# The final norm's gain row loaded by ten transfers on ten semaphores, in a transformer block on one core

## The chip, the cores and the metric

One Trainium2 chip, one core of it, and one launch. The metric is the device time of the kernel in microseconds (us), lower is better. Three runs of the kernel before gave 469.45, 469.94 and 470.28 us, with a median of 469.94. Engines are named as the profile names them: PE is the matrix engine (TensorE), PEld its weight load, DVE is VectorE, ACT is ScalarE, POOL is GpSimd, and SP is SyncE, which here only issues DMA transfers and waits. A `q` behind a name (DVEq, SPq) is the sequencer of that engine, which runs waits, branches and DMA issues.

## The reference

256 tokens of 1024 values pass one layer and a final norm, all in float32:

- x is normalised and projected; a differential attention branch and a gated delta-net branch are gated, merged, projected, and added to x;
- x is normalised again and goes through a mixture of 32 experts (4 groups of 8, the best 2 of the best group for each token), each with gate and up matrices 1024x256 and a down matrix 256x1024; the weighted sum is added to x;
- the last step, the one that the change touches:

```python
def rms_norm(x, gain):
    xf = x.astype(jnp.float32)
    y = xf * lax.rsqrt(jnp.mean(xf * xf, axis=-1, keepdims=True) + EPS)
    return (y * gain.astype(jnp.float32)).astype(x.dtype)
...
    return rms_norm(x, norm_final_gain)
```

`norm_final_gain` is one row of 1024 float32 values, 4096 bytes.

## The kernel before

There is no tiling framework: each engine has a function that writes its instructions in order (`sync_program`, `gpsimd_program`, `scalar_program`, `tensor_program`, `vector_program`), and engines meet only by semaphores. A DMA transfer adds 16 to its semaphore when it has landed, a compute instruction adds 1. Tokens lie on the 128 partitions, in two tiles (t = 0, 1).

The first 230 us are the two branches. Then the 32 experts run as 32 units, eight groups of four. The weights of an expert are three transfers of 1 MB (gate, up, down), issued by SP into seven slots of SBUF. SP issues a reload when the slot is used up (`gateup_used`, `experts_used`), in the loops of lines 394 to 418. The last expert's transfers are those of lines 423, 403 (for the one before it) and 429, in two halves of 512 KB.

Behind them, at line 433, SP issues the load of the gain row: one transfer of 128 partitions, each of which gets the same 4096 bytes, so 512 KB. Its semaphore is `gfin_loaded`, and it is gated by `gateup_used` >= 27 because it goes into a slot's memory. SP then issues only the two stores of the output (line 440), each when its half-rows are ready (`out_left_ready`, `out_right_ready`).

On ACT, DVE and PE all expert code stands in `by_count` (lines 810 to 822): nested If and Else over the largest number of tokens that an expert has, with four versions of the loops. Here the first version runs, and at its end each engine branches (line 813) over the other three.

Behind that branch stands the end of the kernel on DVE (lines 2026 to 2035). For each tile t it waits for ACT's first sum of squares (`squares_done`), makes the mean of it (line 2029), multiplies the left half with the gain (line 2030, which ACT or POOL will scale), waits for ACT's root (line 746), takes the reciprocal (line 2032), and scales and multiplies the right half (line 2034). POOL scales the left half of tile 0 (line 499), ACT that of tile 1 (line 754), behind POOL's by `out_left_ready`. ACT makes the sums of squares from PSUM (line 739) as PE's last matmuls (line 1297) deliver them, and these stand inside the branch on ACT.

Nine semaphores are used for early loads and are then idle: `first_loaded` (it has 16 when its load has landed), `x_loaded0` (16), `x_loaded1` (16), `lambda_loaded` (64), `blocks_loaded` (16), `vectors_loaded` (64), `inverse_loaded` (32), `A_stored` (32), `consts_loaded` (48). The waits for them in the first 260 us are of the form "at least", and all of them are passed long before line 433.

Of the kernel before, what the change touches and what calls it, by code (L numbers as in the profile page):

```python
# [22 lines left out]
P = 128  # L23
# [23 lines left out]
EARLY = (4, 2)  # L47
WARM = 5
BIG = 1e30
LAMBDA_INIT = 0.2  # L50


# [240 lines left out]
def sync_program(sp, c, io):  # L293

    s = c.s
# [124 lines left out]
    e, i, had = EXPERTS - 1, loads - 1, sum(EARLY) * HID  # L420
# [6 lines left out]
    for half, sem in enumerate((f"down{e % SLOTS}", "last_down")):  # L427
# [2 lines left out]


    sp.wait_ge(s["gateup_used"], EXPERTS - SLOTS + 2)
    sp.dma_start(c.gfin, io["norm_final_gain"].rearrange("(a d) -> a d", a=1).partition_broadcast(P)
                 .rearrange("p a d -> p (a d)")).then_inc(s["gfin_loaded"], 16)

    outv = io["out"].rearrange("b (t p) d -> p (b t) d", p=P)
# [373 lines left out]
def by_count(eng, largest, windows):  # L810

    (m0, n0), (m1, n1), (m2, n2), (_, n3) = PATHS
    with eng.If(largest <= m0):
        windows(n0)
    with eng.Else():
        with eng.If(largest <= m1):
            windows(n1)
        with eng.Else():
            with eng.If(largest <= m2):
                windows(n2)  # L820
            with eng.Else():
                windows(n3)
# [628 lines left out]
def vector_program(v, c, io):  # L1451
    s = c.s
    n = [0]

    def chain(ins):
        n[0] += 1
        ins.then_inc(s["dve_chain"], 1)

    def settle():
        v.wait_ge(s["dve_chain"], n[0])  # L1460
# [7 lines left out]
    def side(name):  # L1468
        v.wait_ge(s["side_ready"], SI[name] + 1)
        return c.side[side_pair(name)]  # L1470
# [235 lines left out]
    def maxima(qt):  # L1706

        nk = P * (qt + 1)
        for m in range(2):
            ps = side(f"s{qt}{m}").rearrange("p (h k) -> p h k", h=H)  # L1710
            chain(v.memset(ps[0:CHUNK, :, nk - CHUNK:nk], -BIG))
            settle()
# [35 lines left out]
    def new_values(n_):  # L1748

        rows = slice(CHUNK * (n_ % 2), CHUNK * (n_ % 2) + CHUNK)  # L1750
        dst = c.vn[n_ // 2][rows]
        u = c.u[rows, n_ // 2]
        if n_ == 0:
            v.tensor_copy(dst, u).then_inc(s["vn_ready"], 1)
        else:
            ps = side(f"ws{n_}")[rows, 0:512].rearrange("p (h f) -> p h f", h=H)
            v.tensor_tensor(dst, u, ps, ALU.subtract).then_inc(s["vn_ready"], 1)
            v.wait_ge(s["vn_ready"], n_ + 1)
            v.sem_inc(s[f"side_free{side_pair(f'ws{n_}')}"], 1)
# [24 lines left out]
    settle()  # L1784
    chain(v.tensor_scalar(c.lamw[:, 0:1], c.lamw[:, 0:1], LAMBDA_INIT, None, ALU.subtract))
    new_values(0)
# [13 lines left out]
    def head_norm(squares, ss, sq_flat, root):  # L1800

        v.wait_ge(s[squares], 1)
        chain(v.tensor_reduce(ss, sq_flat.rearrange("p (a f) -> p a f", a=8), AX_X, ALU.add))
        settle()
        v.tensor_scalar(ss, ss, 1.0 / P, EPS, ALU.mult, ALU.add).then_inc(s[root], 1)
        v.wait_ge(s[root], 2)
        chain(v.reciprocal(ss, ss))
        settle()
    new_values(3)
    attended(1)  # L1810

    chain(v.tensor_scalar(c.subln, c.subln, 1.0 - LAMBDA_INIT, None, ALU.mult))
    head_norm("oa_squares", c.ra, c.flat["Yb"], "oa_root")
# [31 lines left out]
    v.wait_ge(s["iota_ready"], 1)  # L1845
    chain(v.tensor_scalar(c.below, c.below, -BIG, None, ALU.mult))
    v.wait_ge(s["rank_masks_ready"], 1)
# [175 lines left out]
                alone(grp, ends(grp), False)  # L2023
    by_count(v, largest, windows)

    v.wait_ge(s["gfin_loaded"], 16)
    for t in range(NT):
        v.wait_ge(s["squares_done"], 2 * t + 1)
# [83 lines left out]
def build(nc, io):  # L2112
    with ExitStack() as ctx:
        c = lay_out(nc, ctx)

        c.A_stored = nc.dram_tensor("stored_A", (4 * H * (CHUNK * CHUNK + CHUNK),), F32, kind="Internal").ap()
        c.inverses_stored = nc.dram_tensor("stored_inverses", (2, 2 * H, P, BLOCK), F32, kind="Internal").ap()
        block = ctx.enter_context(nc.Block())

        @block.sync  # L2120
        def _(sp):
            sync_program(sp, c, io)

        @block.gpsimd
        def _(pool):
            gpsimd_program(pool, c, io)

        @block.scalar
        def _(act):
            scalar_program(act, c, io)  # L2130

        @block.tensor
        def _(pe):
            tensor_program(pe, c, io)

        @block.vector
        def _(v):
            vector_program(v, c, io)
# [24 lines left out]
```

## Time and profile before

| what | value |
|---|---|
| median of 3 runs | 469.94 us (469.45 to 470.28) |
| the profiled execution's own time | 470.17 us |
| its span, first to last instruction | 468.4 us |
| PE busy | 437.4 us (93%) |
| DVE, ACT, POOL busy | 202.0, 122.8, 12.5 us |
| mean granted TensorE clock | 0.971 of 2.4 GHz |
| bytes by SP's queue (q1) | 135.22 MB, 73.1% of 16 engines' span |

The span leaves out 1.8 us of the profiled execution's time. Busy shares are averages over stages with different limits, so the table says little about the last 30 us, where the change lies. For these the chain of waits and the timeline are read: each line of the chain is a start in us from the span's start, a length in us, and what was running or being waited for.

### The profile page before, as it was taken

The page shows a single profiled execution, that of the slowest core. Times are in us where ns is not written, and L with a number is a line of the kernel's source. Part 1 is how long each engine was busy: PE and PEld are TensorE (multiplying, and loading weights), DVE is VectorE, ACT ScalarE, POOL GpSimd, SP SyncE. Part 2 cuts the span into 40 slices and gives each one's busy share as a digit, 9 for nine tenths or more (in the row PEclk, how much of TensorE's full clock was granted, in tenths as well). Part 3 has the DMA queues.
Part 4 walks back from the last instruction along what each step waited for, and adds up shares of the span by engine and source line. Part 5 has one row for each costly group of instructions (what it writes and reads, how often), then busy time and mean ns, then how long its engine had stood idle before and what let it go on. Part 6 is the DMA issues. An engine that isn't in the chain of part 4 may idle for free.

```text
span 468.4 us, 10279 instructions
## 1 busy us (share of the span) xinstructions
PE 437.4 (93%) x4337; PEld 328.4 (70%) x4337; DVE 202.0 (43%) x568; ACT 122.8 (26%) x313; POOL 12.5 (3%) x37
## 2 busy tenths in 40 slices
PE   9999999999999999999999999999997977797683
PEld 8885688874888888888645777768684745665351
DVE  1376367996343551613200654344463123413224
ACT  5002522001132312220012733324242212312134
POOL 6010100000000000000000000000000000000001
PEclk9999999999999999999999999999999787989898
DMA  8969957706504042255598989999999999999982
GB/s 310 407 212 332 411 193 254 278 26 211 183 11 171 23 157 62 118 180 181 195 421 372 348 333 422 418 417 420 419 420 419 422 418 418 421 420 421 415 332 99
DMA packets 38193, 136.87 MB, mean 292 GB/s; under 512 B 9600, under 2 KB 9920, under 8 KB 26240
## 3 DMA queue, kind: packets, MB, share of 16 engines
q1 hardware_dynamic: 33776, 135.22, 73.1%
q10 hardware_dynamic: 4368, 0.95, 1.1%
q8 instruction: 36, 0.59, 0.5%
q14 instruction: 13, 0.11, 0.1%
HBM read 134.59 MB, written 1.57 MB: 291 GB/s over the span
## 4 chain that ended last, share of the span: by engine, by line
PE 65%; DMA 20%; DVE 9%; SPq 3%; issue 2%; ACT 1%; POOLq 0%; ACTq 0%; DVEq 0%
PE ps L890 23%; DMA arena<-in_moe_w_up 12%; PE ps L1268 8%; PE ps L1131 6%; PE ps L1146 6%; DMA ring<-in_moe_w_up 6%; PE ps L1321 3%; PE ps L1311 3%; PE ps L1226 2%; DVE arena L1645 2%; DVE arena L1642 2%; SPq L398 2%; DMA arena<-in_w_in 2%; PE ps L917 2%; PE ps L1276 1%
## 5 line engine op out<-in xcount | busy, mean ns | idle before, releaser
L890 PE MATMUL ps<-arena 128*128 128x256 f32 (+1 forms) x640 | 157.0, 403 | 0.4 <-DMA arena<-in_w_in 0.4
L890 PEld LDWEIGHTS ps<-arena 128*128 128x128 f32 x640 | 119.8, 190 | 29.9 <-issue 14.9
L1268 PE MATMUL ps<-arena 128*32 128x128 f32 x1072 | 41.9, 299 | 13.1 <-DMA arena<-in_moe_w_up 12.9
L1268 PEld LDWEIGHTS ps<-arena 128*32 128x32 f32 x1072 | 32.5, 117 | 20.5 <-DMA arena<-in_moe_w_up 15.3
L1268 PE MATMUL ps<-ring,arena 128*32 128x128 f32 x912 | 34.1, 293 | 7.1 <-DMA ring<-in_moe_w_up 7.1
L703 ACT ACTIVATE gains<-ps 32x256 f32<-32x256 f32 x62 | 23.3, 376 | 56.2 <-PE ps L1311 55.8
L1268 PEld LDWEIGHTS ps<-ring,arena 128*32 128x32 f32 x912 | 26.8, 114 | 12.2 <-DMA ring<-in_moe_w_up 8.1
L1947 DVE TENSOR_TENSOR masks<-ps,masks 128x64 f32<-128x64 f32 x32 | 7.2, 225 | 59.9 <-ACT masks L684 59.7
L1963 DVE COPY arena<-ps 32x256 f32<-32x256 f32 x62 | 25.8, 416 | 11.2 <-PE ps L1311 10.3
L1146 PE MATMUL ps<-arena 128*128 128x512 f32 x64 | 28.3, 595 | 0.0
L1226 PE MATMUL ps<-masks,arena 128*128 128x128 f32 x224 | 28.3, 287 | 0.0
L1226 PEld LDWEIGHTS ps<-masks,arena 128*128 128x128 f32 x224 | 26.9, 200 | 1.8 <-issue 1.8
L1131 PE MATMUL ps<-arena 128*128 128x256 f32 x128 | 28.0, 379 | 0.0
L1131 PEld LDWEIGHTS ps<-arena 128*128 128x128 f32 x128 | 24.2, 190 | 3.3
L1146 PEld LDWEIGHTS ps<-arena 128*128 128x128 f32 x64 | 11.9, 190 | 13.4 <-issue 13.4
L588 ACT ACTIVATE arena<-ps 128x1024 f32<-128x1024 f32 x7 | 7.2, 1023 | 50.9 <-PE ps L890 31.4
L1311 PE MATMUL ps<-arena,masks 128*32 128x256 f32 x256 | 17.0, 382 | 0.1
L690 ACT ACTIVATE masks<-ps 64x64 f32<-64x64 f32 x32 | 6.9, 217 | 37.8 <-PE ps L1276 37.8
L1311 PE MATMUL ps<-ring,masks 128*32 128x256 f32 x240 | 15.9, 382 | 0.0
L1837 DVE TENSOR_TENSOR arena<-arena,ps 128x1024 f32<-128x1024 f32 x4 | 4.9, 1221 | 24.7 <-PE ps L1131 24.7
L1321 PE MATMUL ps<-arena,rw 128*128 128x512 f32 x28 | 15.3, 630 | 0.0
L1932 DVE TENSOR_TENSOR arena<-ps,small 128x512 f32<-128x512 f32 x8 | 5.5, 692 | 22.7 <-PE ps L1226 21.1
(286 smaller groups left out, 453.6 us busy)
## 6 DMA issues: line engine op xcount, KB each, us to landing
arena<-in_w_in SPq DMA_DIRECT2D x9, 2048.0 KB, 7.9
arena<-in_moe_w_gate SPq DMA_DIRECT2D x16, 1024.0 KB, 24.0
arena<-in_moe_w_up SPq DMA_DIRECT2D x16, 1024.0 KB, 25.2
arena<-in_moe_w_down SPq DMA_DIRECT2D x16, 1024.0 KB, 23.9
ring<-in_moe_w_down SPq DMA_DIRECT2D x15, 1024.0 KB, 26.6
ring<-in_moe_w_gate SPq DMA_DIRECT2D x14, 1024.0 KB, 23.3
ring<-in_moe_w_up SPq DMA_DIRECT2D x14, 1024.0 KB, 24.8
arena<-in_w_out SPq DMA_DIRECT2D x2, 2048.0 KB, 7.8
```

Of the source, the lines that this page charges most:

```text
L398: sp.dma_start(flat[slot], src[:, e, :].rearrange("p a f -> p (a f)")).then_inc(s[f"gateup{slot}"], 16)
L703: last = act.activation(stacked(c, i, q), down_out(c, i, q), ACT.Copy)
L890: last = pe.matmul(out, lhs, rhs, start=(k == 0 and (i > 0 or part % 2 == 0)), stop=(k == KD - 1), skip_group_check=(i == 0))
L917: last = pe.matmul(out(ps, i, m), lhs(t, h, m), rhs(t, h, m), start=True, stop=True)
L1131: last = pe.matmul(blk(branch_out(c, half), b, TOK), w[:, k, (4 * half + b) * P:(4 * half + b + 1) * P], yT[:, k, :], start=(k == 0), stop ...
L1146: last = pe.matmul(c.ps[:, 4 + 2 * t + half, :], mg, w[:, k, :], start=(k == 0), stop=(k == KD - 1))
L1226: last = pe.matmul(gather_out(c, k), c.h2[:, t, k, :], c.oh[:, t, :], start=(t == 0), stop=(t == NT - 1))
L1268: last = pe.matmul(c.ps[ROWS * q:ROWS * (q + 1), i % 2, 0:P], c.Hg[:, k, ROWS * i:ROWS * (i + 1)], w[:, :, start:start + 127:2], start=(k ...
L1311: last = pe.matmul(down_out(c, i, q), c.actT[i % 2][:, kk * ROWS:(kk + 1) * ROWS], c.down_w[slot][:, kk, 256 * q:256 * (q + 1)], start=(kk ...
L1321: last = pe.matmul(y_out(c, half, t), c.S_e[:, t * P:(t + 1) * P], c.Y[half], start=False, stop=False, skip_group_check=True)
L1642: chain(v.tensor_tensor(outer, c.block[:, w:BLOCK, j:j + 1].to_broadcast([BLOCKS, n_, w]), c.inverse[:, j:j + 1, 0:w].to_broadcast([BLOCKS ...
L1963: last = v.tensor_copy(stacked(c, i, q), down_out(c, i, q))
```

## The change

The one transfer becomes ten. The first nine load 1, 3, 4, 5, 8, 10, 12, 6 and 15 partitions (64 together), each on one of the nine idle semaphores, and the tenth loads the other 64 partitions on `gfin_loaded`. All stand at the same place of SP's program, behind the same gate. DVE waits for all ten before the final norm. The total is 512 KB as before.

```diff
+GAIN_ROWS = ((1, "first_loaded", 16), (3, "x_loaded0", 16), (4, "x_loaded1", 16), (5, "lambda_loaded", 64), (8, "blocks_loaded", 16), (10, "vectors_loaded", 64),
+             (12, "inverse_loaded", 32), (6, "A_stored", 32), (15, "consts_loaded", 48))
...
     sp.wait_ge(s["gateup_used"], EXPERTS - SLOTS + 2)
-    sp.dma_start(c.gfin, io["norm_final_gain"].rearrange("(a d) -> a d", a=1).partition_broadcast(P)
+    row = 0
+    for n, sem, _ in GAIN_ROWS:
+        sp.dma_start(c.gfin[row:row + n], io["norm_final_gain"].rearrange("(a d) -> a d", a=1).partition_broadcast(n)
+                     .rearrange("p a d -> p (a d)")).then_inc(s[sem], 16)
+        row += n
+    sp.dma_start(c.gfin[row:], io["norm_final_gain"].rearrange("(a d) -> a d", a=1).partition_broadcast(P - row)
                  .rearrange("p a d -> p (a d)")).then_inc(s["gfin_loaded"], 16)
...
     by_count(v, largest, windows)
 
+    for _, sem, had in GAIN_ROWS:
+        v.wait_ge(s[sem], had + 16)
     v.wait_ge(s["gfin_loaded"], 16)
```

## Rows read from the trace of the kernel before

**Rows 1.** Page, part 2: mean busy share of the 16 DMA engines, slices of 11.7 us.
```profile
DMA  8969957706504042255598989999999999999982
```

**Rows 2.** Chain of waits from 456 us: start us, us, what.
```profile
458.18 0.42 DVE gains L1955
458.60 1.98 issue
460.59 0.02 DVEq L2028
460.61 0.06 issue
460.67 0.15 DVE small L2029
...
460.85 0.70 DVE arena L2030
...
461.69 1.62 POOLq L2113
...
463.33 0.04 ACTq L753
463.37 0.05 issue
```

**Rows 3.** Timeline of SP: start us, us, engine line op out<-in.
```profile
9.67 1.39 SPq L339 DMA_DIRECT2D small<-in_gdn_dt_bias  x1
11.10 0.63 SPq L339 DMA_DIRECT2D gains<-in_diff_subln_gain  x1
...
23.80 0.58 SPq L339 DMA_DIRECT2D gains<-in_diff_lambda_q  x1
...
27.07 0.47 SPq L349 DMA_DIRECT2D rw<-in_moe_w_group  x1
...
30.99 4.95 SPq L351 DMA_DIRECT2D small<-in_norm_ffn_gain  x1
...
424.60 2.21 SPq L423 DMA_DIRECT2D ring<-in_moe_w_gate  x1
...
435.88 4.44 SPq L429 DMA_DIRECT2D arena<-in_moe_w_down  x1
440.36 4.30 SPq L433 DMA_DIRECT2D arena<-in_norm_final_gain  x1
```

**Rows 4.** Page, part 6: DMA issues, count, KB each, median us from issue to landing.
```profile
out_y<-arena SPq DMA_DIRECT2D x2, 512.0 KB, 3.6
arena<-in_norm_final_gain SPq DMA_DIRECT2D x1, 512.0 KB, 17.3
gains<-in_diff_subln_gain SPq DMA_DIRECT2D x1, 64.0 KB, 13.8
small<-in_gdn_dt_bias SPq DMA_DIRECT2D x1, 2.0 KB, 15.0
```

**Rows 5.** Line 429: us from issue to landing of its two transfers.
```profile
DMA to landing us min/median/max: 20.6/21.0/21.5
```

**Rows 6.** Line 813: the branch out of the If; ns min/median/max.
```profile
L813 PEldq COMPARE_BRANCH  x2: 89/1878/3666, 268.1 to 458.7; - x2
L813 DVEq COMPARE_BRANCH  x2: 47/51/55, 268.9 to 457.8; - x2
```

**Rows 7.** Timeline of ACT and DVE at the end.
```profile
459.92 0.19 ACT L739 ACTIVATION_READ_ACCUMULATOR arena<-ps 128x1 f32 x1
...
461.46 0.15 DVE L2032 RECIPROCAL small<-small 128x1 f32<-128x1 f32 x1
```

**Rows 8.** Lines 1492, 1493, 515: semaphore instructions of DVE and a 48-partition issue; ns.
```profile
L1492 DVEq EVENT_SEMAPHORE  x1: 21/21/21, 16.5 to 16.5; - x1
L1493 DVEq EVENT_SEMAPHORE  x1: 50/50/50, 16.6 to 16.6; - x1
L515 ACTq DMA_DIRECT2D cst_in<-in_gdn_conv_w x1: 338/338/338, 1.5 to 1.5; - x1
```

## The prediction, as made before the changed kernel was run

> **What bounds the kernel now.** I read the page's DMA slices first, then the chain of waits over the last 14 us, then SP's timeline for the transfers, then the landings. The slices show nine tenths or more from about 290 us to 445 us [rows 1]: the expert weights' bytes set the time there, and the gain row is the last thing behind them. From 450 us on the chain is made of compute [rows 2]. Its last part is: DVE's copy of the last expert's output ends at 458.60, then 1.98 us of "issue" (DVE waits for nothing that the profile shows), then the wait at line 2028, the mean (460.67), the left half's product (460.85 to 461.54), then POOL's scaling of the left half, ACT's, and the stores. The reader is to see that DVE's program from line 2026 on stands on the path that sets the end, and that the gain row does not: it is issued at 440.36 and lands 17.3 us later, at 457.7 [rows 3, 4], and DVE takes up line 2028 at 460.59 only. The slack is 2.9 us.
>
> Why is DVE late? ACT's first sum of squares is complete at 459.92 + 0.19 = 460.11 [rows 7], so the wait at 2028 was 0.48 us overdue when DVE came to it. Ahead of it stands the branch at 457.8 over the other three versions, 0.05 us by itself on DVE; on PE the branch of the same line lasts 3.67 us, from 458.7 [rows 6]. I read the 1.98 us as DVE getting its code from behind the branch. The Trainium skill says so as a rule (Runtime: NRT & Kernel Launch, section "Instruction fetch mechanics"): a taken branch to code outside the window that is held must fetch that page first, and the engine stands still. The rows agree, and this makes what follows the branch on DVE exposed: by the other reading the added waits would cost nothing.
>
> **The change part by part.**
>
> *The nine waits on DVE.* They are added between the branch and line 2028. How are waits packed? At lines 1489 to 1495 DVE has four waits (lines 1490 to 1493) ahead of one instruction. The rows show two semaphore instructions there, of 21 ns and 50 ns [rows 8]. Lines 750 to 753 on ACT have three waits and the chain shows one semaphore instruction of 0.04 us [rows 2]. So an instruction takes one wait itself, a semaphore instruction of 21 ns carries one, and a longer one carries two. Before, lines 2026 and 2028 were two waits: one semaphore instruction and one on line 2029. After, there are eleven: one on line 2029, ten in five semaphore instructions. Price: 0.02 + 0.06 = 0.08 us for the single one (460.59 to 460.67), 0.04 + 0.05 = 0.09 us for a double one (463.33) [rows 2]; DVE's double one is 0.012 us longer than ACT's, so 0.10. Sum: 5 x 0.09 to 0.10 less 0.08 = +0.37 to +0.43 us. Bounds: 0 if the waits pass during the 1.98 us, and 10 x 0.08 - 0.08 = +0.72 us if each wait is an instruction of its own. I take +0.4, from the rows nearest to it. All of it goes on: the product at 460.85 ends at 461.54 and DVE's work behind it is in order, POOL starts behind it, ACT waits for POOL, the stores wait for both [rows 2]. Queued behind the waiting instructions is the whole final norm of both tiles. If all ten transfers are there, nothing else changes.
>
> *The first piece on SP.* It inherits gate and place of the old transfer. That one's issue lasted 4.30 us, and the one before it 4.44 [rows 3]; whether this is the gate or a queue that is full, the first piece bears it again and ends at about 444.7.
>
> *The other nine issues.* A short issue takes 0.5 to 0.6 us with others still in flight: seven of them, with the gaps behind them, fill 23.80 to 27.54, so 0.53 us each [rows 3]. An issue of 48 partitions costs 0.34 us on ACT [rows 8]. So nine take 9 x 0.53 = 4.8 us, to 449.5. Behind them on SP stand only the stores, 14 us later: this costs nothing as long as the last issue is over by about 457. Other bound: while the queue is full an issue takes 2.1 to 2.2 us even for a quarter of the size (2.21 at 424.60), once even 4.95 for a transfer of 4 KB behind two with many small pieces [rows 3]. Nine at 2.15 would be 19 us. I take 0.53, since the pieces are short, and keep the other end for the rival.
>
> *The landing.* The weights ahead are not moved. The last of them lands at 435.88 + 20.6 = 456.4 [rows 3, 5], the gain row 1.2 us behind it. The pieces queue there too, the bytes are the same. What each landing costs beside its bytes: two small loads issued 1.4 us apart behind the same backlog land at 9.67 + 15.0 = 24.7 and 11.10 + 13.8 = 24.9, so 0.2 us apart [rows 3, 4]. Nine more such steps are 1.8 us: the last landing is 457.7 to 459.5, before 460.6. Cost nothing; the cover is DVE's branch, and each us that the last piece is later than about 460.9 is a us of the total.
>
> Which engines carry the pieces no row shows. The Trainium skill (DMA: Bandwidth & Descriptors, section on why a DMA increments its semaphore by 16) says that a transfer goes over as many of the 16 engines, at most 16, as divides its outer size, and the lowest-numbered ones. By it the first DMA engine gets one row of each of eight pieces, a quarter of the single row, and 4 rows of the last 64, so 12.25 instead of 8. With 1.2 us for 8 rows that is 0.65 us more, a landing at 458.3 instead of 457.7, and the sum stays as it is.
>
> *The reused semaphores.* Their earlier waits ask for "at least" and are passed 180 us or more before; no instruction is added there. Nothing.
>
> **Sum.** +0.4 us on the span (468.4 to 468.8), +0.4 on the profiled execution's own 470.17, so 470.6. That execution is 0.23 above the median 469.94 of the runs, so for the median I expect 470.3 us. What this measurement can tell from no change is 0.2%, 0.94 us; +0.4 (0.09%) is below that.
>
> **The rivals.**
>
> *Hidden waits* (chance 0.12). If the 1.98 us is a wait that the added ones can run inside, the time stays 469.9. For it: the profile names no reason for the stall. Against it: the sum of squares was there at 460.11, and the branch on PE.
>
> *A full queue holds the pieces back* (0.14, the rival on the slower side). Place: SP's issues from 444.7. Price: 2.15 us each until the weights are through at 456.4, so five of them (to 455.4), then four at 0.53 to 457.5. The last piece lands on an empty queue after 3.6 us, as the stores of 512 KB do [rows 4], so at 461.1 at the latest; a later throttle (one more 4.3 us as at 435.88) makes it 465. It decides once the landing is behind 460.9: 0.2 us in the first form, 4.1 in the second, and I price this rival at the middle, 2.1 us with the 0.4 of the waits, 472.0. For it: the issues of 2.1 to 6.3 us that fill SP's timeline from 413 on. Against it: the seven quick ones from 23.80.
>
> *Each landing costs more than a queue shows* (0.03). If each of nine landings cost 0.9 us, the last would be at 465.8, 4.9 late: 475.2. Against it: the 0.2 us above.
>
> *Code placement* (0.03 each way). Five more instructions on DVE behind the branch, nine on SP; if they pass an edge at which code is fetched, DVE stands once more for about 2 us (472.3), or comes earlier (by the 0.48 us that it was late, 469.5, and no faster unless PE's and ACT's shares move too).
>
> That the ten do not do what one did is not among them: the rows 0 to 63 and 64 to 127 are all covered, each once.
>
> **How the numbers follow.** Forecast 0.65, its own range 469.5 to 471.1 (0 to 0.72, and 0.4 us for the spread of the runs). Within 0.2%: 0.61 of the forecast's 0.65, the hidden waits' 0.12, and of the queue rival's mild form 0.02: 0.75. Slower: 0.03 of the forecast, 0.12 of the queue rival, 0.03 of the landings and 0.03 of the code: 0.21. Faster: 0.03 of the code and 0.01 of the forecast, 0.04. The range reaches up to the queue rival's price and below to the fastest run: 469.3 to 471.9.
>
> **What would show each step.** Between the branch and line 2029 five DVE semaphore instructions of 0.05 us in place of one, and line 2029 at about 461.1. Nine short SP issues from 444.7 to 449.5, and the longest landing among the ten at 457.7 to 459.5. The interval from line 2029 to the end of the span the same as before, 7.7 us. Wrong if: SP issues of 2 us or more between the pieces and DVE's wait ending with a landing; or more than five semaphore instructions on DVE.

## The result, and the profile after

The changed kernel takes 471.94 us (median of 4 runs, 471.63 to 472.46) against 469.90 for the kernel before (469.45 to 470.28). The ratio is 1.0040, with a 95% interval of 1.0028 to 1.0052: 0.4% slower, +1.3 to +2.4 us. The forecast was 470.3 and "within 0.2%". The time lies beyond that bound and at the very end of the range, 471.9. The profiled execution took 471.64 us with a span of 469.9, so +1.5 us on the 470.17 and 468.4 of before. It is one of the two shortest of the four runs, so the rows account for 1.5 us, not for the median's 2.0. In what follows a median is of all executions; one of 548 to 876 us in each of e2, e7, e9, e10 and e12 ran in a slow state, counts in that median, and is left out of the ratio.

The chain of waits of the changed kernel from 435 us on (start us, us, what). Lines 1294, 1962, 2037 and 2038 are lines 1287, 1955, 2028 and 2029 of before.

```profile
435.56 22.08 DMA arena<-in_moe_w_down
457.65 0.04 issue
457.69 1.08 PE ps L1294 x8
458.77 0.02 issue
458.80 0.06 DVE gains L1962
458.86 2.79 issue
461.65 0.05 DVEq L2034
461.70 0.06 issue
461.75 0.05 DVEq L2034
461.80 0.05 issue
461.85 0.05 DVEq L2034
461.90 0.05 issue
461.95 0.05 DVEq L2035
462.00 0.05 issue
462.05 0.05 DVEq L2037
462.10 0.05 issue
462.15 0.15 DVE small L2038
462.30 0.03 issue
462.33 0.70 DVE arena L2039
```

Two things differ from [rows 2]. First, five double semaphore instructions stand ahead of the mean, 0.05 us each and 0.10 apart. The mean starts 0.50 us after the first of them, where it was 0.08: +0.42 us. Second, all of it starts at 461.65 and not at 460.59: +1.06 us. Together 1.48 us, and that is the whole of the span's 1.5: from the mean to the end of the span it is 7.7 us in both.

Where is the 1.06 from? The chain now ends in a transfer that was not in it: the last half of the last expert's down matrix, issued at 435.56, lands at 457.65. The weights' two landings, by the line that issues them in the changed kernel (us from issue to landing; [rows 5] has those of before, 20.6 for the last half, which landed at 456.43):

```profile
DMA to landing us min/median/max: 22.1/22.5/22.8
```

The last half is 1.2 us late. PE waits for it with the second half of line 1294, which ends at 458.77. Before, these matmuls had both halves' data and ended at 457.71:

```profile
456.68 1.04 PE ps L1287 x16
457.71 0.02 issue
```

PE is 1.06 us later, so DVE's last copy is, so is its branch, and the 2.8 us behind the branch are then paid from there. The branches in the changed kernel (ns min/median/max, first and last start us; those of before are in [rows 6]):

```profile
L820 PEldq COMPARE_BRANCH  x2: 89/1886/3682, 267.8 to 459.3; - x2
L820 DVEq COMPARE_BRANCH  x2: 47/51/55, 268.6 to 458.8; - x2
```

From DVE's branch to its next instruction it is 2.8 us in both (457.8 to 460.59 before, 458.8 to 461.65 after).

SP in the changed kernel (start us, us, engine line op out<-in xcount), and the last piece of the gain row on the page (KB, us from issue to landing):

```profile
433.37 6.48 SPq L431 DMA_DIRECT2D arena<-in_moe_w_down  x2
439.90 7.11 SPq L437 DMA_DIRECT2D arena<-in_norm_final_gain  x9
447.05 0.52 SPq L440 DMA_DIRECT2D arena<-in_norm_final_gain  x1
```

```profile
arena<-in_norm_final_gain SPq DMA_DIRECT2D x1, 256.0 KB, 12.0
```

Ten pieces are issued within 7.7 us, none of them behind a stall of 2 us or more, and the one issued last lands at 459.05, 2.6 us before DVE asks. The landings of the other nine are not in the profile, but none of DVE's five semaphore instructions stands still. So the gain row is not waited for. It harms the weights ahead of it. The windows around 451 us show how (us from:to, length; busy us of PE, PEld, DVE, ACT, POOL with counts; granted clock; DMA share, GB/s). Before:

```profile
445.00:451.00 6.00, 6.00 (x93) 3.63 (x96) 1.25 (x3) 1.19 (x4) 0.00 (x0) 1.00 1.03 407
451.00:453.00 2.00, 1.83 (x42) 1.11 (x38) 1.34 (x4) 1.25 (x5) 0.00 (x0) 1.00 0.90 355
```

The changed kernel:

```profile
445.00:451.00 6.00, 6.00 (x101) 3.74 (x103) 1.25 (x3) 1.42 (x5) 0.00 (x0) 1.00 1.02 406
451.00:453.00 2.00, 1.82 (x49) 1.22 (x45) 1.35 (x4) 1.19 (x4) 0.00 (x0) 1.00 0.96 248
453.00:455.00 2.00, 1.01 (x36) 0.73 (x28) 0.51 (x2) 0.91 (x2) 0.00 (x0) 1.00 0.72 218
```

Until 451 us nothing differs, though all ten pieces are issued by 447.6. From then on the DMA engines are as busy as before and move 248 GB/s in place of 355. Bytes per busy share, 394 before (355 / 0.90) and 258 after, is the number that I follow through the experiments: packets take 1.5 times as long. No instruction of DVE, ACT or PE explains it; their busy times in this window are the same within 0.1 us (DVE 1.34 and 1.35, ACT 1.25 and 1.19, PE 1.83 and 1.82).

The trace also has each packet's size and duration, and there the two loads can be told apart: the gain row goes in 128 packets of 4096 bytes, the weights of this stretch in packets of 2048 and 8192. In the kernel before, the gain row's packets run from 450.9 to 457.2 us, among the weights', the last of which ends at 455.9. So both are in flight together there too, and it does no harm. A weight packet of 2048 bytes that starts between 451 and 453 us takes 87 ns in the median there and 126 in the changed kernel; one of 8192 bytes takes 314 and 488. It is the weights' own packets that slow.

### The profile page after: what moved, and what is told of

Same layout as the page of the kernel before. It is cut to its first block, busy times and chain, and to the rows that moved or that the text cites. A ratio compares the mean times of both kernels' runs of the same rounds, so it can differ in the third digit from the quotient of the medians.

```text
span 469.9 us, 10292 instructions
## 1 busy us (share of the span) xinstructions
PE 441.1 (94%) x4337; PEld 330.9 (70%) x4337; DVE 201.9 (43%) x568; ACT 122.9 (26%) x313; POOL 12.5 (3%) x37
## 4 chain that ended last, share of the span: by engine, by line
PE 67%; DMA 19%; DVE 8%; issue 2%; SPq 1%; ACT 1%; POOLq 0%; ACTq 0%; DVEq 0%
PE ps L897 23%; PE ps L1275 9%; DMA arena<-in_moe_w_up 6%; DMA ring<-in_moe_w_up 6%; PE ps L1138 6%; PE ps L1153 6%; DMA arena<-in_moe_w_down 5%; PE ps L1233 4%; PE ps L1318 4%; PE ps L1328 3%; DVE arena L1652 2%; DVE arena L1649 2%; DMA arena<-in_w_in 2%; PE ps L924 2%; PE ps L1283 1%
## 5 line engine op out<-in xcount | busy, mean ns | idle before, releaser
L1275 PE MATMUL ps<-arena 128*32 128x128 f32 x1072 | 43.4, 307 | 12.5 <-DMA arena<-in_moe_w_up 12.1
L1233 PEld LDWEIGHTS ps<-masks,arena 128*128 128x128 f32 x224 | 28.0, 207 | 2.0 <-issue 2.0
L1233 PE MATMUL ps<-masks,arena 128*128 128x128 f32 x224 | 29.4, 293 | 0.0
L1153 PEld LDWEIGHTS ps<-arena 128*128 128x128 f32 x64 | 11.9, 190 | 13.4 <-issue 13.4
```

The source lines that it names most:

```text
L1153: last = pe.matmul(c.ps[:, 4 + 2 * t + half, :], mg, w[:, k, :], start=(k == 0), stop=(k == KD - 1))
L1233: last = pe.matmul(gather_out(c, k), c.h2[:, t, k, :], c.oh[:, t, :], start=(t == 0), stop=(t == NT - 1))
L1275: last = pe.matmul(c.ps[ROWS * q:ROWS * (q + 1), i % 2, 0:P], c.Hg[:, k, ROWS * i:ROWS * (i + 1)], w[:, :, start:start + 127:2], start=(k ...
```

## The experiments

Two costs are to be explained: the waits (+0.42) and the late weights (+1.06). The theories on the second, by their letters:

- P: transfers of fewer than 128 partitions slow whatever is in flight beside them (first put more narrowly: because a piece's rows are neighbouring partitions).
- N: the number of transfers or of packets does it. S: the ten semaphores do. U: small pieces put more rows on some DMA engines than on others. Q: one source row read by many small transfers. R: chance, the late landing is one execution's.
- On the waits, H: they are hidden in the stall behind the branch.

Every experiment was timed beside the kernel before on the same chip; its times there were medians of 470.13 to 470.29 us. The edits of e2, e3, e4, e7 and e11 are shown against the changed kernel, those of e5, e6, e8, e9, e10 and e12 against the kernel before; where only new lines are shown they stand in place of the load of the gain row.

**e1, the changed kernel again** (no edit).

> The changed kernel once more, for a second profile. Theory W (small pieces slow the weight packets that are still under way, and the five added DVE semaphore instructions cost 0.4 us): the last down half lands about 1.2 us later than in the kernel before, packets in the stretch around 451 to 454 us take 1.3 to 1.6 times as long, the time is about 2 us above the kernel before. Rival R (the slow packets were chance in one profiled execution): they are gone in this profile, and the time is about 0.5 us above the kernel before.

471.98 us (471.46 to 472.55) against 470.13, ratio 1.0038 (1.0026 to 1.0049). The last half lands after 21.8 us, and the window of 451 to 453 us has 252 GB/s at 0.98. R is refuted: another execution, the same two findings. (e1 to e4 share a chip, e5 to e8 a second, e9 to e12 a third; the late weights appear on all three.)

**e2, only the waits.** One transfer as before; nine waits for values already reached.

```diff
-    row = 0
-    for n, sem, _ in GAIN_ROWS:
-        sp.dma_start(c.gfin[row:row + n], ...).then_inc(s[sem], 16)
-        row += n
-    sp.dma_start(c.gfin[row:], ... .partition_broadcast(P - row) ...
+    sp.dma_start(c.gfin, ... .partition_broadcast(P) ...
...
-        v.wait_ge(s[sem], had + 16)
+        v.wait_ge(s[sem], had)
```

> One transfer as before; DVE keeps the nine waits, at values that the nine semaphores have long reached. Theory W: +0.4 us against the kernel before (five semaphore instructions of 0.10 us in place of one of 0.08), the last down half lands as before. Rival H (waits hidden in the stall behind the branch): 0.0 us.

470.96 us, ratio 1.0016 (1.0001 to 1.0030): +0.8 us with an interval of 0.05 to 1.4, which holds the 0.4 and just excludes 0. The weights are on time (20.3 us; 334 GB/s at 0.85, so 393 per share). The chain behind its branch:

```profile
457.37 3.02 issue
460.39 0.05 DVEq L2029
...
460.78 0.05 DVEq L2032
460.83 0.05 issue
460.89 0.15 DVE small L2033
```

The waits run behind the stall, not in it: 0.50 us from the first to the mean again. H is refuted.

**e3, ten transfers on one semaphore.**

```diff
-                     ... .then_inc(s[sem], 16)
+                     ... .then_inc(s["gfin_loaded"], 16)
...
-    for _, sem, had in GAIN_ROWS:
-        v.wait_ge(s[sem], had + 16)
-    v.wait_ge(s["gfin_loaded"], 16)
+    v.wait_ge(s["gfin_loaded"], 16 * (len(GAIN_ROWS) + 1))
```

> The ten transfers as in the change, all on gfin_loaded, DVE waits once for 160. Theory W: about 1.6 us above the kernel before, 0.4 below the change; the last down half lands late as in the change. Rival S (the nine reused semaphores or their waits are what costs): as the kernel before, 0.0 us.

471.54 us, ratio 1.0024 (1.0011 to 1.0037). The weights are as late as in the change (22.1 us; 239 GB/s at 0.97). S is refuted. On the same chip it is 0.44 us below e1, from which it differs by the nine semaphores and their waits alone: the third reading of 0.4.

**e4, ten slices of columns**, each over all 128 partitions (102 columns, 408 bytes a row), on the ten semaphores.

```diff
+    gain = io["norm_final_gain"].rearrange("(a d) -> a d", a=1)
+    for i, sem in enumerate([g[1] for g in GAIN_ROWS] + ["gfin_loaded"]):
+        a, b = 102 * i, 102 * (i + 1) if i < len(GAIN_ROWS) else D
+        sp.dma_start(c.gfin[:, a:b], gain[:, a:b].partition_broadcast(P) ... .then_inc(s[sem], 16)
```

> Ten transfers of all 128 partitions, each 102 (the last 106) columns wide, on the ten semaphores, with the ten waits. Theory P (it is the shape that costs: few partitions, so that several DMA engines write where one does otherwise): weights land as before, +0.4 us for the waits alone. Rival N (it is the number of transfers): the last down half lands 1.2 us late here too, +1.6 us or more.

470.60 us, ratio 1.0012 (0.9998 to 1.0026), so +0.5 us, in line with the waits alone, though the interval reaches 0. The profile has the waits: from the first of the five semaphore instructions (460.35) to the mean (460.85) it is 0.50 us. The last half lands after 20.3 us. As many transfers as in the change and ten times the rows of the one transfer of before, and the weights are on time: N is refuted. The window has 294 GB/s at 0.83, 354 per share, but here the gain row goes in packets of 408 bytes, so that number can't be compared; the weights' packets of 2048 bytes can, and take 84 ns. One thing is not equal: the ten issues take 13.4 us and end at 453.5, six us later than in the change. e12 is the counterpart without that gap.

**e5, eight transfers of 16 neighbouring partitions**, one semaphore. By the rule that the prediction quotes, 16 rows are one for each of the 16 DMA engines, and U needs them uneven.

```diff
+    for i in range(8):
+        sp.dma_start(c.gfin[16 * i:16 * i + 16], ... .partition_broadcast(16) ...).then_inc(s["gfin_loaded"], 16)
```

> Eight transfers of 16 neighbouring partitions each, one semaphore, one wait for 128. Every DMA engine gets one row of every transfer, 8 in all as in the kernel before. Theory P (several engines write into neighbouring partitions at once, and that slows every packet in flight): packets from 451 us on are slow, the last down half lands 1 us or more late, +1.2 to +1.6 us. Rival U (it is that the low-numbered engines get more rows than the others): all engines get the same here, the weights land at 456.1 to 456.4 as before, 0.0 us.

471.23 us, ratio 1.0019 (1.0009 to 1.0029); landing after 21.6 us. U is refuted. The whole of this trace is 0.4 us later, so the window catches less of it (334 GB/s, but at a share of 1.07: 312). From 452 to 454 us its weight packets of 2048 bytes take 134 ns, where the kernel before has 84.

**e6, the same with every eighth partition** (rows i, i+8, ... in one transfer).

```diff
+        sp.dma_start(c.gfin[i:P:8], ... .partition_broadcast(16) ...).then_inc(s["gfin_loaded"], 16)
```

> Eight transfers of 16 partitions that lie 8 apart (i, i+8, ...), one semaphore, one wait. As many transfers, rows and engines as with neighbouring partitions. Theory P: with each transfer spread over all partitions the packets are faster than with neighbouring ones, the last down half lands within 0.5 us of the kernel before's 456.4. Rival N (the number of small transfers, or k of 16 with one row each, costs): the same lateness as with neighbouring partitions.

471.31 us, ratio 1.0022 (1.0012 to 1.0032); 21.9 us; 256 GB/s at 1.00. As late as with neighbouring rows. My narrow form of P fell here: which partitions a piece has does not matter.

**e7, rows of x as the source.** The ten pieces take their rows from 128 different rows of x, so the gain is left out and x stands in its place; one semaphore.

```diff
-        sp.dma_start(c.gfin[row:row + n], io["norm_final_gain"]... .partition_broadcast(n) ...
+        sp.dma_start(c.gfin[row:row + n], io["x"][0, row:row + n, :]).then_inc(s["gfin_loaded"], 16)
...
+    sp.dma_start(c.gfin[row:], io["x"][0, row:P, :]).then_inc(s["gfin_loaded"], 16)
```

> The ten transfers with one semaphore, but each partition loads a row of x of its own (4096 bytes each, 128 different rows) in place of the one gain row; the final norm therefore multiplies with x and not with the gain. Theory P (destination): as with the gain row, the last down half lands about 1.2 us late, +1.6 us. Rival Q (several engines read the same 4 KB of HBM at once): with rows of their own the packets are fast again, the weights land at 456.4, 0.0 us.

471.58 us, ratio 1.0027 (1.0017 to 1.0037); 22.0 us; 269 GB/s at 1.02. Q is refuted.

**e8, two transfers of 64 partitions**, one semaphore.

```diff
+    for i in range(2):
+        sp.dma_start(c.gfin[64 * i:64 * i + 64], ... .partition_broadcast(64) ...).then_inc(s["gfin_loaded"], 16)
```

> Two transfers of 64 partitions, one semaphore, one wait for 32. Theory P: each engine writes 4 neighbouring rows, two engines share what one writes in a transfer of 128; a part of the lateness, 0 to 0.6 us. Rival N (number of transfers): 2 of 10, at most 0.2 us. Rival U: 0.0 us.

471.68 us, ratio 1.0033 (1.0023 to 1.0043): +1.5 us where I had expected 0 to 0.6. Two transfers cost as much as ten on one semaphore (e3, 1.4). The landings are the latest of all kernels, and the window is slow:

```profile
DMA to landing us min/median/max: 22.5/22.6/22.8
```

```profile
451.00:453.00 2.00, 1.97 (x58) 1.58 (x54) 0.89 (x3) 1.19 (x4) 0.00 (x0) 1.00 1.04 272
```

So of what these runs vary, what counts is that a transfer has fewer than 128 partitions (1 to 64 here; nothing between 64 and 128 was run); how many pieces there are does not.

**e12, two transfers of 128 partitions**, halves of the columns: the counterpart to e8 (edit on the kernel before).

```diff
+    for i in range(2):
+        sp.dma_start(c.gfin[:, 512 * i:512 * i + 512], ... .partition_broadcast(P) ...).then_inc(s["gfin_loaded"], 16)
```

> Two transfers of all 128 partitions, each half of the columns, one semaphore and one wait for 32: as many transfers and bytes as in two of 64 partitions. Theory P: packets at full speed, last down half at 456.1 to 456.4, 0.0 us. Rival N (two transfers in place of one): +1.5 us as with 64 partitions.

470.17 us, ratio 0.9994 (0.9980 to 1.0007): no difference. Its landings and its window:

```profile
DMA to landing us min/median/max: 20.5/20.9/21.4
```

```profile
451.00:453.00 2.00, 1.96 (x49) 1.31 (x48) 0.43 (x2) 0.66 (x3) 0.00 (x0) 1.00 0.96 372
```

388 per share against e8's 262, with the same count of transfers and of bytes, and weights on time against 2 us late. The weights' packets of 2048 bytes take 87 ns in e12 and 132 in e8. (Its profiled execution, 471.41, is the longest of the nine behind the ratio, and PE was already 1.1 us behind at 451 us, ahead of the window; of it only landing, window and packets are used.)

**e9, the two transfers of 64 behind the weights.** SP waits for the last half first.

```diff
+    sp.wait_ge(s["last_down"], 16)
+    for i in range(2):
+        sp.dma_start(c.gfin[64 * i:64 * i + 64], ... .partition_broadcast(64) ...).then_inc(s["gfin_loaded"], 16)
```

> Two transfers of 64 partitions as before, but SP issues them only when the last down half has landed, so that no weight packet is in flight beside them. Theory P (gain packets with another assignment of engines to partitions slow the weight packets beside them): the last down half lands at 456.1 to 456.4 as in the kernel before; the gain row lands about 3.6 us after that, near 460.1, just before DVE asks; 0 to +0.3 us against the kernel before, 1.3 us below the same two transfers issued early. Rival L (a split load costs by itself, whatever is beside it, or DVE's end is late for another reason): +1.5 us as when issued early.

The weights are on time, as P says (20.5 us). The time is not: 471.73 us, ratio 1.0028 (1.0015 to 1.0041), +1.4 us where I had expected 0 to 0.3. The chain, SP and the window of the pieces in e9:

```profile
458.05 0.42 DVE gains L1958
458.47 3.50 issue
461.97 0.02 DVEq L2031
```

```profile
456.51 1.15 SPq L437 DMA_DIRECT2D arena<-in_norm_final_gain  x2
```

```profile
457.50:460.00 2.50, 1.88 (x7) 0.91 (x6) 0.91 (x3) 1.44 (x4) 0.00 (x0) 1.00 0.76 218
```

The pieces are slow even among themselves: 287 per share, and 212 ns for a packet of 4096 bytes, which takes 159 in the kernel before. Their last packet ends at 460.25 and they land until 460.96. DVE meanwhile stands 3.50 us behind its branch in place of the 1.98 of [rows 2], and once it goes on it waits for nothing more. The 1.5 us move from the weights to the stall. The instruction queue shows where they go. Packets, MB and share of DMA, first in the kernel before from 457.8 to 459.5 us, then in e9 from 457.6 to 459.7, where the data queue is all that moves:

```profile
q14 instruction: 1, 0.01, 1.8%
```

```profile
q1 hardware_dynamic: 142, 0.49, 79.8%
```

Before, the 8 KB packet of instructions starts at 458.75, 1.0 us behind DVE's branch, and so it does in the other profiles with that branch (1.0 to 1.3). In e9 the branch is at 457.62 and the packet starts at 459.79, 2.2 us behind it, when most of the pieces' packets are through; DVE's next instruction follows 2.2 us behind that start, before 1.8. So the fetch is late, by 1.2 us at its start. That it stands behind the pieces' packets fits and is argued. No run has one transfer of 128 partitions at this place, so whether the form of the pieces matters here, or any transfer would do it, is open.

**e10, DVE's final norm inside the branch** (the kernel before; lines 2026 to 2035 moved to the end of `windows`, each version with its own copy). It asks whether the stall is the fetch behind the branch.

```diff
+        v.wait_ge(s["gfin_loaded"], 16)
+        for t in range(NT):
+            ... (the loop's body, unchanged)
...
     by_count(v, largest, windows)
-    v.wait_ge(s["gfin_loaded"], 16)
-    for t in range(NT):
-        ...
```

> The kernel before, with DVE's final norm moved to the end of each version inside the If, so that no branch stands ahead of it. Theory B (DVE stands after the branch until its code is there, 0.46 us past the sum of squares): line 2029's instruction starts at 460.2 in place of 460.67, and the time is 0.3 to 0.5 us lower. Rival O (DVE is held by something else): 0.0 us.

The stall is gone. ACT and DVE in e10:

```profile
459.65 0.19 ACT L739 ACTIVATION_READ_ACCUMULATOR arena<-ps 128x1 f32 x1
...
459.96 0.15 DVE L2027 TENSOR_SCALAR small<-small 128x1 f32<-128x1 f32 x1 [1.62 <-ACT arena L739]
```

DVE's mean starts 0.12 us after ACT's sum (459.84), where it was 0.56 late [rows 2, 7]. The Trainium skill states the rule (Runtime: NRT & Kernel Launch, "Instruction fetch mechanics": a taken branch out of the pages that are held forces a fetch before execution goes on); this run agrees, with 0.44 us of lateness gone and no packet of q14 between 457.8 and 463 us.

Yet the kernel is not faster: 471.11 us, ratio 1.0011 (0.9999 to 1.0023). The mean is 0.71 us earlier than before (459.96 against 460.67), but the reciprocal behind it only 0.34 (461.12 against 461.46 [rows 7]): it waits for ACT's root, and ACT is at its second sum of squares until 460.70. So the two stores are issued 0.3 us earlier, and they land later. The stores on the page, and the instruction queue from 463 to 469 us (packets, MB, share), in e10:

```profile
out_y<-arena SPq DMA_DIRECT2D x2, 512.0 KB, 4.2
```

```profile
q14 instruction: 4, 0.03, 2.1%
```

Before, the stores took 3.6 us [rows 4] and that window had 2 packets of q14 (and one of q8, which in e10 starts at 462.79, ahead of the window). DVE's branch is now at 463.05, and its packet of instructions at 464.0 or 464.3, beside ACT's: the fetch is not saved but moved, to where the stores run. They take 4.2 us here and 3.9 in e11, and 3.4 to 3.8 in the twelve others. That the fetch is what slows them fits and is not separated. The moving of the code bought nothing.

**e11, the same edit on the changed kernel.**

> The changed kernel with the same move. The last down half stays late (about 457.6), but the five semaphore instructions can run right behind DVE's last copy, before ACT's sum of squares at about 460.53. Theory B: the mean starts near 460.6 in place of 462.15, 1.4 to 1.6 us below the changed kernel, about level with the kernel before. Rival O: 0.4 us below at most.

471.31 us, ratio 1.0013 (1.0000 to 1.0026), span 468.9. Its chain:

```profile
435.54 21.90 DMA arena<-in_moe_w_down
457.44 0.04 issue
457.49 1.06 PE ps L1294 x8
...
460.36 0.05 DVEq L2035
460.41 0.05 issue
460.46 0.15 DVE small L2036
```

The weights are late as in the change, but one semaphore instruction is left on the path: the other four ran at 458.6 to 458.95, while DVE had nothing to do. The mean is at 460.46 and not at 462.15. 1.7 us earlier there, 1.0 in the span: 0.35 are given back at ACT's root (the reciprocal is at 461.60 against 462.94) and 0.3 at the stores (3.9 us against 3.6), both as in e10. So the expectation came true for the mean, not for the time, which I had put about level with the kernel before and which is 1.0 us above it. What the waits cost depends on what the engine would do in their place.

None of the twelve beats the kernel before.

## Why the prediction was right in part, and which step failed

**The waits: right.** Five double semaphore instructions, 0.10 us apart, +0.42 us (forecast 0.37 to 0.43; 5 x 0.10 - 0.08 is 0.42, not 0.43), in the profile of the change, as e3 against e1 (0.44), and within e2's interval. The hidden waits, the first rival, did not come.

**The landing: the step that failed.** It says "The weights ahead are not moved. The last of them lands at 435.88 + 20.6 = 456.4". It was 457.65. I let the pieces queue behind the weights and asked only when the pieces land; that part came (459.05 for the one issued last, forecast 457.7 to 459.5), and the rival by which each landing costs 0.9 us fell with it. That transfers issued behind the weights could slow those ahead had no term and no rival: it was put at nothing, and it costs 1.06 us. The trace of before offered a reason to ask: the weights take 21 to 27 us to land while an issue is over in a few, and the gain row's packets run among the last weights' from 450.9 us on, not behind them. [Rows 5] gives the 1.06 us its place: PE's last matmuls follow that landing at once, and it had no slack.

**The cover: right, and with a gap.** The gain row had 2.9 us of slack and has 2.6. But I counted slack for the transfer that changed and not for those beside it.

**The issues.** I had the first piece bear the 4.30 us again and the others take 0.53. All nine took 0.32 to 1.19 us, 7.1 in all. The first has one partition; a first piece of 16 (e5, e6) or 64 (e8) does take 4.3 us at that place. Here the end, 447.6, is near the forecast 449.5. The full queue, the rival on the slower side, did not come: no issue took 2 us and DVE waited for no landing. That its price, 472.0, lies near the measured 471.94 is chance, and by the prediction's own terms the price was 472.5 (469.94, the middle of 0.2 and 4.1, and the 0.4 of the waits). The range reached as far as 471.9 by that rival alone, so that the time falls at its end is luck and says nothing for the working.

**The rule on the engines.** By the Trainium skill's rule (DMA: Bandwidth & Descriptors, "Why a DMA increments its semaphore by 16 and not by 1") the prediction put more rows on the first DMA engines, for a landing 0.65 us later (458.3). No row tells the engine of a packet, so the rule itself is not shown here. e5 has 16 rows a piece, even by that rule, and is as late: the unevenness is not what costs.

**Code placement** did not come as a rival: 2.8 us from branch to next instruction in both.

**The sum.** +0.4 forecast; +0.42 and +1.06 found, 1.5 us in the span. The medians say 2.0 (this kernel) and 1.85 (e1), with an interval in e1 of 1.2 to 2.3 that holds 1.5. Whether the missing 0.3 to 0.5 us is anything stays open.

**Shown and only argued.** In this kernel, with 512 KB of gain row behind the last weights, shown: transfers of 1 to 64 partitions beside the weights, in eight profiles (the change, e1, e3, e5 to e8, e11), make the last weights land 1.0 to 1.9 us later (21.6 to 22.5 us); transfers of 128 partitions, one, two or ten of them (before, e2, e4, e10, e12), do not (20.3 to 20.7). It is not chance, the number, the semaphores, the source, the evenness of rows, or which partitions a piece takes. The weights' packets of 2048 bytes, started from 451 to 453 us, take 126 to 146 ns in seven of the eight (e5, 0.4 us later as a whole, has 134 from 452 to 454) and 84 to 87 in the five and in e9. Why is only argued. The Trainium skill (DMA: Bandwidth & Descriptors, "The descriptor swizzle") says that in a transfer to 128 partitions each DMA engine writes through one SBUF port of its own. A smaller transfer dealt out over 16 engines would then put several engines on one port and hold up the weights' packets there. The slowing of the weights' packets fits that; no row names a port or an engine, and the transfers of fewer partitions also hand the rows to other engines, which no run holds apart from the ports.

## What to carry to other kernels

A transfer issued last is not for that behind all others: its packets can run among those of the transfers ahead (here from 450.9 us on). Ask what it does to their landing, above all if the last of them has no slack. Keep small loads that run beside a stream of weights in the same 128-partition form as the stream, and cut them by columns if they must be cut. Here waits behind a stall were paid in full (e2) and those ahead of work that is late anyway were free (four of five in e11); and a transfer or a code fetch moved to a quiet place is to be checked for what it then stands beside.

## What the runs showed of the hardware

- Two transfers of 64 partitions in place of one of 128: bytes per busy share fall from 394 to 262 GB/s, and weights issued 4.5 us earlier land 1.9 us later (e8); a weight packet of 2048 bytes takes 132 ns in place of 87. On their own, behind the weights, the two run at 287 (e9).
- In this kernel waits are packed two to a semaphore instruction and one on the instruction itself: eleven make five semaphore instructions of 0.10 us on DVE.
- Issues of 1 to 15 partitions beside a full stream took 0.32 to 1.19 us here, while at the same place the first issue of 16 (e5, e6), 64 (e8) or 128 partitions [rows 3] took 4.3.
- A branch over other code costs DVE 2.8 us until its next instruction, of which 1.0 passes until an 8 KB packet of instructions starts; with the two transfers of 64 in flight it is 4.4 us, 2.2 of them until that packet starts (e9: branch at 457.6, next at 461.97). With that fetch moved beside the stores, these take 4.2 us in place of 3.6 (e10).
